# A hybrid decoder layer in one kernel: the first FFN pair computed in token halves, gate and up in turn

## What is computed

```python
    merged = jnp.sum(gate.astype(proj.dtype) * proj, axis=2)
    return merged @ w_out
...
def swiglu_ffn(h, w_gate, w_up, w_down):
    return (jax.nn.silu(h @ w_gate) * (h @ w_up)) @ w_down
...
        x = x + hybrid_mixer(h, w_in[l], ...)
        h = rms_norm(x, ffn_norm[l])
        x = x + swiglu_ffn(h, w_ffn_gate[l], w_ffn_up[l], w_ffn_down[l])
```

## Time and profile before

| | us |
|---|---|
| median of 3 runs | 760.38 |
| lowest, highest | 760.29, 760.74 |
| profiled execution, its own time | 760.82 |
| profiled execution, span | 759.0 |
| TensorE busy | 751.5 |
| VectorE busy | 591.5 |
| ScalarE busy | 404.8 |

### The profile page before, as it was taken

One profiled execution on the slowest core, in us unless ns is written; L12 is line 12 of the kernel. 1 busy time (PEld: TensorE's weight loads), 2 busy tenths in 40 slices (PEclk: granted clock), 3 DMA queues, 4 the chain that ended last, 5 costly groups with the idle time before them and its releaser, 6 DMA issues.

```text
span 759.0 us, 11534 instructions
## 1 busy us (share of the span) xinstructions
PE 751.5 (99%) x4542; PEld 664.0 (87%) x4542; DVE 591.5 (78%) x816; ACT 404.8 (53%) x603; POOL 104.6 (14%) x130
## 2 busy tenths in 40 slices
PE   8999999999999999999999999999999999999998
PEld 8988888988888888888888799999888999999886
DVE  5636989878788966425978799889988888888991
ACT  6645546456663554545348565565544556565530
POOL 7100040457203221221230000000000000000000
DMA  8362223221133123317236444336073333339202
GB/s 270 103 194 68 93 62 112 67 101 55 56 112 110 57 59 110 111 55 276 85 94 173 122 167 122 113 108 242 1 250 111 112 112 112 111 112 313 75 28 83
DMA packets 67876, 89.54 MB, mean 118 GB/s; under 512 B 3108, under 2 KB 52592, under 8 KB 67696
## 3 DMA queue, kind: packets, MB, share of 16 engines
q1 hardware_dynamic: 66224, 85.60, 34.6%
q0 software_dynamic: 1456, 3.09, 2.0%
q10 hardware_dynamic: 144, 0.13, 0.1%
HBM read 81.99 MB, written 4.19 MB: 114 GB/s over the span
## 4 chain that ended last, share of the span: by engine, by line
PE 91%; DVE 3%; issue 2%; ACT 1%; DMA 1%; POOL 1%; DVEq 0%; POOLq 0%; SPq 0%
PE bank L2305 14%; PE bank L2307 14%; PE bank L2306 14%; PE bank L2743 8%; PE bank L2745 8%; PE bank L2744 8%; PE bank L2804 5%; PE bank L2808 5%; PE bank L2806 5%; PE bank L2686 1%; PE bank L2685 1%; PE bank L2684 1%; DMA w_lo<-plain 1%; PE bank L2394 1%; PE bank L2563 1%
## 5 line engine op out<-in xcount | busy, mean ns | idle before, releaser
L2305 PE MATMUL bank<-h_hi,w_hi 128*128 128x512 f32 (+1 forms) x352 | 134.6, 383 | 0.2 <-DVE w_lo L1557 0.2
L2307 PE MATMUL bank<-h_hi,w_lo 128*128 128x512 f32 (+1 forms) x352 | 133.7, 380 | 0.0
L2306 PE MATMUL bank<-h_lo,w_hi 128*128 128x512 f32 (+1 forms) x352 | 133.6, 380 | 0.0
L1485 DVE TENSOR_TENSOR w_lo<-raw,w_hi 128x2048 fp32r<-128x2048 f32 x31 | 73.4, 2369 | 41.3 <-ACT w_hi L873 33.3
L2743 PE MATMUL bank<-t_hi,w_hi 128*128 128x256 f32 x320 | 88.5, 276 | 0.4 <-ACT w_hi L1312 0.4
L2744 PE MATMUL bank<-t_lo,w_hi 128*128 128x256 f32 x320 | 88.3, 276 | 0.0
L2745 PE MATMUL bank<-t_hi,w_lo 128*128 128x256 f32 x320 | 88.3, 276 | 0.0
L2305 PEld LDWEIGHTS bank<-h_hi,w_hi 128*128 128x128 f32 x352 | 66.2, 188 | 12.6 <-ACT w_hi L936 0.4
L2307 PEld LDWEIGHTS bank<-h_hi,w_lo 128*128 128x128 f32 x352 | 66.2, 188 | 12.6
L2306 PEld LDWEIGHTS bank<-h_lo,w_hi 128*128 128x128 f32 x352 | 66.2, 188 | 12.1
L2743 PE MATMUL bank<-f_hi,w_hi 128*128 128x256 f32 x240 | 66.3, 276 | 0.0
(11 more groups left out here) (349 smaller groups left out, 1841.4 us busy)
## 6 DMA issues: line engine op xcount, KB each, us to landing
raw<-in_w_in_dram SPq DMA_DIRECT2D x26, 1024.0 KB, 5.1
raw<-in_w_ffn_up_dram SPq DMA_DIRECT2D x11, 1024.0 KB, 5.1
raw<-in_w_ffn_gate_dram SPq DMA_DIRECT2D x10, 1024.0 KB, 5.1
raw<-in_w_ffn_down_dram SPq DMA_DIRECT2D x7, 1024.0 KB, 5.0
raw<-in_w_branch_dram SPq DMA_DIRECT2D x4, 1024.0 KB, 4.9
b<-in_w_ffn_down_dram SPq DMA_DIRECT2D x4, 1024.0 KB, 6.4
x_sb<-in_x_dram SPq DMA_DIRECT2D x6, 512.0 KB, 4.7
o<-in_w_out_dram SPq DMA_DIRECT2D x3, 1024.0 KB, 9.8
```

The lines of the kernel that those rows point to most:

```text
L1485: vec.tensor_tensor(w_lo[:, at], raw[:, c % 2, 0:n], w_hi[:, high].bitcast(F32), ALU.subtract)\
L2305: mm(dst, l_hi, r_hi, start=start, stop=False)
L2306: mm(dst, l_hi, r_lo, start=False, stop=False)
L2307: return mm(dst, l_lo, r_hi, start=False, stop=stop)
```

## The change

Gate and up of the first pair are computed in the order gate, up for tokens 0 to 255, then gate, up for tokens 256 to 511, all in 256-column products. Gate's tiles go to banks 2 and 3 instead of 0 and 1; up's stay in two banks for both halves. The transposes of token tiles 2 and 3 move into up's first half. Up gets a place of its own, `p1_hi` and `p1_lo`; both copies are made early by ScalarE, and the whole is added to the negated one by an accumulating DMA on GpSimd, as for gate. VectorE's subtraction for up is gone. On ScalarE, squares move, all use one half of `two`, and gate's two copies now stand together; on VectorE the addition (6, 1) moves ahead of the variance of tile 2. SyncE's hand-over of `lo_ready` is done for both chunks.

```diff
+        P1_AT = in_phase(L0 + 40 * KB, (F_PHASE + 64) % LINE)
+        p1_hi = place("p1_hi", [P, CHUNK], F32R, at=P1_AT)
+        P1_LOW = in_phase(P1_AT + 8 * KB, (F_PHASE + 192) % LINE)
+        p1_lo = place("p1_lo", [P, CHUNK], F32R, at=P1_LOW)
...
             for c in range(PLAIN[1], F11 + 1):
                 if c == WINO[0]:
                     sp.wait_ge(S["out_lo"], OT4 + 1)
-                    sp.wait_ge(S["plain0_added"], 16)
-                    sp.wait_ge(lo_ready, PLAIN[0])
+                if c in WINO[:2]:
+                    sp.wait_ge(S["plain_added"], 16 * (c - PLAIN[1]))
+                    sp.wait_ge(lo_ready, c - 2)
                     sp.sem_inc(lo_ready, 1)
                 load(c)
...
-            pool.wait_ge(S["out_seeded"], 7)
             at = w_at(PLAIN[0])
-            pool.dma_start(w_lo[:, at:at + CHUNK], plain0[:, :], accum_op=ALU.add).then_inc(S["plain0_added"], 16)
+            for n, (low, whole) in enumerate(((w_lo[:, at:at + CHUNK], plain0[:, :]), (p1_lo[:, :], raw[:, PLAIN[1] % 2, :]))):
+                pool.wait_ge(S["out_seeded"], 7 + n)
+                if n:
+                    pool.wait_ge(S["plain_added"], 16)
+                pool.dma_start(low, whole, accum_op=ALU.add).then_inc(S["plain_added"], 16)
...
             out_seed(3, 0, x_sb[:, 2, HALF:D])
             sum_parts("S3")
+            square(0, 0, 1)
+            square(1, 0, 2)
             out_seed(3, 1, x_sb[:, 3, HALF:D])
...
             nact.activation(w_hi[:, at + HIGH_OFF:at + HIGH_OFF + CHUNK], plain0[:, :], ACT.Copy).then_inc(hi_ready, 1)
-            square(0, 0, 1)
-            square(1, 0, 2)
+            nact.activation(w_lo[:, at:at + CHUNK], plain0[:, :], ACT.Copy, scale=-1.0).then_inc(S["out_seeded"], 1)
             square(0, 1, 3)
             take_root(slice(0, 1))
-            nact.activation(w_lo[:, at:at + CHUNK], plain0[:, :], ACT.Copy, scale=-1.0).then_inc(S["out_seeded"], 1)
             square(1, 1, 4)
             take_root(slice(1, 2))
+            act.wait_ge(raw_ready[PLAIN[1] % 2], 16 * raw_count(PLAIN[1]))
+            act.wait_ge(S["out_tile"], out_tile(3, 1))
+            nact.activation(p1_hi[:, :], raw[:, PLAIN[1] % 2, :], ACT.Copy).then_inc(hi_ready, 1)
+            nact.activation(p1_lo[:, :], raw[:, PLAIN[1] % 2, :], ACT.Copy, scale=-1.0).then_inc(S["out_seeded"], 1)
             square(2, 1, 5)
+            h2_high(0)
             square(3, 1, 7)
-            h2_high(0)
+            h2_high(1)
             h2_copy(0)
-            h2_high(1)
...
             act.wait_ge(S["out_tile"], len(OUT_ORDER))
-            split(PLAIN[1])
...
-                gated(0, j, bank[(fill_at[PLAIN[0]] + j) % 2])
+                gated(0, j, bank[2 + j])
...
             h2_low(1)
+            out_add(6, 1, 3, 0, 8)
             variance(2, 7)
             inverse_root(slice(2, 3))
             scaled(2)
-            out_add(6, 1, 3, 0, 8)
...
-            split(PLAIN[1])
             block_sums()
...
+            def plain_part(up, half):
...
+                pe.wait_ge(hi_ready, c + 1)
+                pe.wait_ge(lo_ready, c + 1)
                 pe.wait_ge(S["h2_lo_ready"], TT * (half + 1) - 1)
+                pe.wait_ge(S["x1_taken"], (8, OUT_ADDS)[up])
                 for j in range(CT):
+                    b = bank[(fill_at[c] + j) % 2] if up else bank[2 + j]
...
+                        if up and half == 0 and k == 0:
+                            turn_h2(2 + j)
                     if half == 1:
                         last.then_inc(filled, 1)
...
+            for half in range(2):
+                for up in range(2):
+                    plain_part(up, half)
```

More of the change, by code:

```diff
@@ L550, in hybrid_layer @@
             o11_in right_half_in o21_in plain0_in out_t_made out_hi out_lo out_s_made out_s_hi out_s_lo
-            out_seeded out_tile first_added v0_added v1_added plain0_added rstd_ready h_scaled h_last_scaled h_turned h_hi_ready h_lo_ready vec_turned ws_ready ws_turned
+            out_seeded out_tile first_added v0_added v1_added plain_added rstd_ready h_scaled h_last_scaled h_turned h_hi_ready h_lo_ready vec_turned ws_ready ws_turned
             iw_turned iw_ready mix_in second_hi second_lo ik_moved ik_hi_ready ik_lo_ready first_lo iq_hi_ready iq_stacked iq_lo_stacked idx_filled relu_ready relu_used
@@ L1252, in square @@
                 act.wait_ge(S["x1_taken"], added)
-                if n >= 2:
-                    act.wait_ge(S["squares_summed"], 4 + n - 1)
+                if n:
+                    act.wait_ge(S["squares_summed"], 4 + n)
                 late = TT * (half == (1 if t < 2 else 0))
-                nact.activation(two[:, n % 2, :], x_sb[:, t, half * HALF:(half + 1) * HALF], ACT.Square,
+                nact.activation(two[:, 1, :], x_sb[:, t, half * HALF:(half + 1) * HALF], ACT.Square,
                                 accum_out=sums[:, late + t:late + t + 1]).then_inc(S["squares_summed"], 1)
@@ L2692, in _ @@
                     turn_h2(1 - t)
[L2694 to L2697, removed]
+            def plain_part(up, half):
+                c = PLAIN[up]
+                at = w_at(c)
+                c_hi, c_lo = (p1_hi[:, :], p1_lo[:, :]) if up else (w_hi[:, at + HIGH_OFF:at + HIGH_OFF + CHUNK],
+                                                                    w_lo[:, at:at + CHUNK])
                 cols = slice(half * SEQ // 2, (half + 1) * SEQ // 2)
+                pe.wait_ge(hi_ready, c + 1)
+                pe.wait_ge(lo_ready, c + 1)
                 pe.wait_ge(S["h2_lo_ready"], TT * (half + 1) - 1)
+                pe.wait_ge(S["x1_taken"], (8, OUT_ADDS)[up])
                 for j in range(CT):
-                    b = take_bank(fill_at[first] + j)
-                    pe.wait_ge(S["x1_taken"], (9, OUT_ADDS)[j])
+                    b = bank[(fill_at[c] + j) % 2] if up else bank[2 + j]
                     for k in range(KT):
@@ L2705, in _ @@
                             pe.wait_ge(S["h2_lo_ready"], TT * (half + 1))
[L2706 to L2713, removed]
+                        w = slice(k * CW + j * P, k * CW + (j + 1) * P)
+                        begin, end = k == 0 and half == 0, k == KT - 1
+                        mm(b[:, cols], c_hi[:, w], f_hi[:, k, cols], start=begin, stop=False, skip_group_check=True)
+                        mm(b[:, cols], c_hi[:, w], f_lo[:, k, cols], start=False, stop=False, skip_group_check=True)
+                        last = mm(b[:, cols], c_lo[:, w], f_hi[:, k, cols], start=False, stop=end, skip_group_check=True)
+                        if up and half == 0 and k == 0:
+                            turn_h2(2 + j)
                     if half == 1:
                         last.then_inc(filled, 1)
[L2717 to L2725, removed]
+            for half in range(2):
+                for up in range(2):
+                    plain_part(up, half)
             B11, B21, B22 = (LOWER, T1ST), (UPPER, T1ST), (UPPER, T2ND)
```

## The result

The changed kernel takes **765.97 us** (median of 6 runs, 763.97 to 767.50) against 760.83 (6 runs, 760.29 to 761.24): a ratio of 1.0066, interval 1.0050 to 1.0081. It is 5.1 us slower. The forecast was 762.4 with a range up to 765.5: the direction came true, the size did not, and the time lies half a microsecond outside the range. The forecast was built on 760.38, the median of three runs of before; with the six it would have been 762.8. The profiled execution took 766.43 us with a span of 764.3, where that of before had 759.0.

The account below looks back on a forecast made before the run. VectorE's gapless run was taken to bound the kernel at product S1, by 0.58 us. A start moved to 430.7, plus 18.4, less 447.09 gave +2.0 us; on 760.38 that made 762.4 us, range 761.0 to 765.5.

Parts of the forecast that it names:

- What goes away: VectorE loses up's low part (2.29 us) and a 1.02 us wait; TensorE's waits at 433.13 and before tile 3's transposes vanish.
- point (a): Sign in the profile: no TensorE wait at the bank of gate's second tile or before the transposes of tile 3.
- point (b): Sign in the profile: TensorE waits about 3 us before product S1.
- The main term: WINO[0]'s weight sums wait for gate's end, 18.4 us after S, the first gate matmul: +0.9 us with S unchanged.
- point (c): Sign in the profile: VectorE idle ahead of the first w_sum, released by a gate matmul at about 449.
- How S moves: First gate matmul (S) slips from 429.60 to 430.7, because ScalarE's early up copies wait for up's load, landing at 421.8.
- The rival that let the load be there in time: Up's load lands by 419.8, first gate matmul about 429.4: +0.7 us, range +0.4 to +1.2; chance 0.22.
- Points (d) and (e): Signs: ScalarE idle before p_hi until up's load at about 421.8; first gate matmul near 430.7.
- The new DMA: GpSimd's accumulating DMA for up's low part, perhaps sharing engines with WINO[0]'s load: cost 0 to 1.6 us, taken as 0.
- Point (f): Sign in the profile: up's first matmul has no wait of its own.
- Gate's own low part: Gate's accumulating DMA, previously 6.9 us, now starts some 3 us earlier and costs nothing.
- Rival 2: Up's load or low part is held back more by accumulating DMA traffic: up to +6 us, low part up to 1.6; chance 0.29.

Follow-up runs that it names:

- e1: Changed kernel, with up's low part made by a VectorE subtraction instead of the second accumulating DMA: 762.93 us, ratio 1.0032.
- e7: e1 plus 28 dummy 256-column products on TensorE ahead of the wait for product S1: 761.63 us, ratio 1.0014.
- e10: e1 with VectorE's seed addition, which product S1 needs, moved ahead of the four weight sums of WINO[1]: 760.63 us, ratio 1.0007.
- e8: Changed kernel with dummy work both before up's first product (24 transposes) and before product S1 (28 products): 764.70 us, ratio 1.0055.
- e4: Changed kernel plus 24 dummy transposes on TensorE before the wait for up's low part: 767.09 us, ratio 1.0081.
- e2: Changed kernel with WINO[0]'s load issued only after up's accumulating DMA has landed: 764.59 us, ratio 1.0041.
- e3: Changed kernel, but gate for all tokens, then up; VectorE waits for up's low part before its block sums: 759.44 us, ratio 0.9982.
- e6: Changed kernel with up's first token half split around gate's second half, and WINO[0]'s load behind up's accumulating DMA: 759.23 us, ratio 0.9982.

## Why the forecast had the sign and not the size

- **The bound** (VectorE's gapless run sets S1, and S1 sets the end): right. The run from w_sum to L2215 stayed at 13.6 us in after, e1 and e7, and span and S1 moved by the same 5.3 us.
- **What goes away**: right. The waits at gate's second tile and at tile 3's transposes are gone, point (a), and S1 waits 3.2 us instead of 0.4, point (b), as forecast.
- **The main term, +0.9 by S + 18.4**: right. e7 measures 0.8, e1's w_sum stands 18.49 us behind its S (429.24), and the waiting row names gate's product, point (c).
- **How S moves, +1.1**: wrong. S stayed at 429.6. Up's load took 8.1 us instead of the 9.9 of before, for which I had assumed no relief and even 0.5 us more; it landed 0.2 us before ScalarE came to `p_hi`. The rival that let the load be there in time had the true condition, at +0.7. Points (d) and (e) failed. So more than half of the forecast 2.0 us came from a term that did not happen, and its error hid a part of what was missing elsewhere.
- **The new DMA, "bounds 0 and 1.6; I take 0"**: this is the step that failed, with 2.5 us in the trace of after and at most 3.1 us by the runs. Point (f) failed with it: up's first product waited 2.4 us. Its two halves should be looked at apart. The landing for the case "one after the other" was worked out as 437.8, and it was 437.52. But the moment by which it is needed was taken from the S' of 430.7 that did not come; from the true 429.6 it is 435.2. A late S would have hidden most of this cost: the two terms could not both be small, and I had priced the second as if the first were certain. And for the value I took the middle of two landings, where two transfers that serialise have no middle.
- **Gate's own low part "costs nothing"**: right for VectorE, wrong for the queue. It met up's load, took 9.7 us (8.4 to 10.1 in the traces of e1 to e10) instead of 6.9, and so released up's low part at 426.5 instead of the 425.8 assumed.
- **The clock**: missing from the sum. One fall cost 1.6 us in the traces, and after gives up at least 1.3 us for it in the median. I had the waits of 3 us in the forecast, and counted them as free because the end did not hang on them.
- **Rival 2** (load or low part held back more) is the one that happened, by its second half. It had been given at most 1.6 for the low part, which kept the top of the range at 765.5. With 0.9, 2.6 (437.8 less 435.2) and one fall of the clock, 1.6, the sum would have been 5.1. That it meets the measured 5.1 so closely is in part luck, since the landing alone moves by 1.9 us between the traces of e8, after and e4. The rival also says that in before gate's transfer never met up's load. It did, from 419.29 to 421.3, and the load kept its pace there: q1 has 21 packets in 419:420 and 22 in 420:421, beside 63.4% of the engines' time for q0.

What stays open: a wait of 3.3 us at S1 is followed by the lower clock in the traces of e2 and e4, and not in those of e1 and after. That it comes in most but not all runs is seen from e1's spread and its closing in e7; what decides it in one run was not found. Nor do the runs say how L and C share the 4.3 us in any run but the profiled one.

## What to carry to other kernels

Two DMAs that one landing releases, one of them accumulating, are to be priced one after the other, with the needed one last, and the moment of need is to be taken from the case in which everything else goes well. A wait of TensorE of 2 to 3 us is not free where nothing hangs on it: look at the granted clock behind it, and at the spread of the runs. Before splitting a product in halves over tokens, ask who waits for the end of the first chunk: here the rest of the change won 1.3 us, and the order of the halves turned that into a loss. And before a dummy filling is read as a price, look whether it ends before the wait that it fills.

## What the runs showed of the hardware

- An accumulating DMA of 1024 KB issued beside a load of the same size took 11.0, 11.4, 11.6 and 11.2 us (after, e3, e4, e8) and 7.5 us alone (e2, e6), while the load paid about 1 us (6.1 in after against 5.1 in the earlier trace rows). In after the smaller one shows it as well: x's 256 KB, issued at 412.71 just behind the load, landed 8.3 us later, where the one of 409.87 took 4.4. Its packets of 2 KB come mainly at 417, behind some three microseconds of the load's; the rows are 414:415 and 417:418:

```profile
q1 hardware_dynamic: 242, 0.25, 83.8%
...
q0 software_dynamic: 74, 0.15, 81.3%
q1 hardware_dynamic: 106, 0.10, 31.1%
```

- TensorE's granted clock fell to 1.2 GHz behind waits of 2.4 us (after) and 3.3 us (e2, e4), each time for some 1.6 us of lost time. With dummy work in the waits it stayed at 1.00 in the traces of e7 and e8; in before, whose longest wait in this stretch is 1.0 us, it stays at 1.00.
